# Moving the FFN's DMA transposes to ScalarE's queue, two more tiles by DMA, and split scores for dilation one

## The chip, the cores and the metric

The kernel runs on one core of a Trainium2 chip. The metric is the time of one launch on the device in microseconds, taken as the median of several runs. One more run was profiled; all rows below come from it.

## What is computed

A trunk of two layers over 256 tokens of width 1024: a sparse attention mixer (NSA) and an FFN, then a dilated attention mixer and an FFN, each with a norm ahead, a norm behind and a residual sum. The parts that matter here, from the reference:

```python
def swiglu(h, w_gu, w_down):
    gu = h @ w_gu
    g, u = gu[..., :D_FF], gu[..., D_FF:]
    return (jax.nn.silu(g) * u) @ w_down

# dilated_mixer: for each (window, dil) of ((128, 1), (512, 4), (2048, 16))
    q = partial_rope(proj[:, :, gi, 0], cos, sin)
    k = partial_rope(proj[:, :, gi, 1], cos, sin)
    v = proj[:, :, gi, 2]
    o, lse = banded_attention(to_residue(q, dil)[:, :, :, None], to_residue(k, dil),
                              to_residue(v, dil), window // dil)
...
    s = jnp.einsum('nqhgd,nkhd->nhgqk', qc, kc).astype(jnp.float32) * scale
```

## The kernel before

Everything is written out by hand: five engine programs (SyncE, GpSimd, ScalarE, VectorE, TensorE), each in a fixed order, tied by semaphores. Tokens come in two tiles of 128, m = 0 and 1. A weight piece (128 x 2048 floats) is loaded by SyncE into a ring of seven slots; ScalarE copies it to a rounded high part `w_hi` (line 719, two halves), VectorE subtracts to get `w_lo` (line 1231), and each product is three single-pass matmuls, hi·hi, hi·lo and lo·hi (`three`, all matmuls at line 1785). Small matmuls of plain float operands (scores, values) are left in full float and are issued by the same helper `mm`.

**FFN.** The hidden width 2816 is cut into FJ = 11 tiles j = 0 to 10. For each (j, m) TensorE makes gate and up (`gu`), ScalarE the silu (986), VectorE the product `hs` (1569). `hs` must be transposed before the down projection can use it. For j = 2 to 9 (`XBAR`) that goes by DMA: GpSimd splits the floats into two 16-bit planes (679), SyncE's queue issues a DMA transpose (474, in `turn_planes`, placed among the weight loads by `turns_before`), GpSimd merges the planes into `ht` (684). For j = 0, 1 and 10 TensorE transposes instead (`ht_turn`, line 1794). ScalarE then copies the high part to `st_hi` (998, `ht_out`; `end_hi` for j = 10), VectorE makes `st_lo` (1575), and TensorE runs `down`. TensorE's order of a step is gu(j, 0), down(j-1, 0), gu(j, 1), down(j-1, 1). The last step is gu(10, 0), down(9, 0) with the transposes of hs(10, 0) in its middle, down(10, 0), gu(10, 1), down(9, 1), down(10, 1).

**Dilated attention.** The heads are taken in four groups g of four. The tiles of a group (projections of q and k for each of the three dilations, `pat` 0 to 2, and of the values) follow each other; in between stand the attention steps of the group before, two heads (a pair) at a time, 16 pairs in all. A q/k tile is evacuated by ScalarE (1079), rotated by VectorE (`dil_rope`, 1663 to 1670), transposed by TensorE (`dil_turn`) into bank 2 or 3, and copied by ScalarE to `qk_t` (1102 to 1111). `dil_scores` makes the scores of a pair: for dilation one a 64x128 by 64x256 product per head in full float, and eight 64x64 products for the other two. VectorE masks (1426), ScalarE takes the exponential (901), VectorE normalises (`norm_unit`, 1459), TensorE transposes the probabilities (`dil_turn_probs`).

Of the kernel before, what the change touches and what calls it, by code (L numbers as in the profile page):

```python
# [39 lines left out]
P = 128  # L40
# [83 lines left out]
N_TURNS = sum(x.kind == QK for x in TILES)  # L124

# [68 lines left out]
def build(nc, x, positions, norm_mix_pre, norm_mix_post, norm_ffn_pre, norm_ffn_post, ffn_w_gu,  # L194
# [3 lines left out]
    with ctx:  # L198
# [25 lines left out]
        probs = sb("probs", [P, 4, 512], at=at_tmp)  # L224
        pair = sb("pair", [P, 2, HK, S], at=at_tmp)
# [211 lines left out]
        rope_parts = sem("rope_parts")  # L437
# [32 lines left out]
        def _(sp):  # L470
            def turn_planes(layer, j, m):

                sp.wait_ge(planes_ready, xbar_no(layer, j, m) + 1)
                sp.dma_start_transpose(planes_t[:, j % 2, m, :, :], planes[:, j % 2, m, :])\
                  .then_inc(planes_turned[m], 16)

            def turns_before(n):

                for layer, first in enumerate((N_FFN0, N_FFN1)):
                    for j in XBAR:  # L480
                        if n == first + 3 * j + 6:
# [2063 lines left out]
```

## Time and profile before

| | us |
|---|---|
| median of 3 runs | 815.26 (815.19 to 816.67) |
| the profiled execution, its own time | 814.93 |
| its span, first to last instruction | 812.9 |
| TensorE matmul busy | 801.4 (99%), 4377 instructions |
| VectorE busy | 511.5 (63%) |
| ScalarE busy | 455.5 (56%) |
| GpSimd busy | 96.7 (12%) |

2.03 us of the profiled execution lie outside its span. TensorE's granted clock was 0.998 of full speed over the span. Matmuls are pipelined, so two of them overlap in the records: a 512-column matmul is recorded with 0.39 us, but the next one starts some 0.23 us after it. What a matmul costs is therefore read from start to start, and idle time from the starts as well.

### The profile page before, as it was taken

How to read it: one execution, taken by the hardware profiler on the slowest of the kernel's cores; microseconds unless marked ns; L12 is line 12 of the kernel's file. 1: busy time of each engine (PE TensorE's matmuls, PEld its weight loads, DVE VectorE, ACT ScalarE, POOL GpSimd, SP SyncE). 2: the span in 40 equal slices, each digit the busy share in tenths (PEclk: the TensorE clock that was granted, in tenths of full speed). 3: DMA queues.
4: the chain of work that ended last, by engine and by line, in shares of the span. 5: the costliest groups of instructions: out<-in, count | busy, mean ns of one | idle time of the engine just before them, and what ended most of it. 6: DMA issues, size and time to landing. Idle time of an engine off the chain costs nothing.

```text
span 812.9 us, 11748 instructions
## 1 busy us (share of the span) xinstructions
PE 801.4 (99%) x4377; PEld 643.5 (79%) x4377; DVE 511.5 (63%) x1073; ACT 455.5 (56%) x879; POOL 96.7 (12%) x159
## 2 busy tenths in 40 slices
PE   9999999999999999999999999999999999999996
PEld 7877675788888888788877878878877888888885
DVE  5966979786646464686565665666568765555444
ACT  7836878764535353575555666555558553535331
POOL 1000005700222222000000000000000012222210
PEclk9999999999999999999999999999999999999999
DMA  9955211166986687558444535363434667767711
GB/s 318 346 186 197 88 54 53 63 223 195 234 216 191 191 244 216 170 194 273 153 160 145 167 115 197 104 206 105 156 110 142 196 226 203 207 184 238 224 32 52
DMA packets 126312, 141.69 MB, mean 174 GB/s; under 512 B 23680, under 2 KB 109744, under 8 KB 126128
## 3 DMA queue, kind: packets, MB, share of 16 engines
q1 hardware_dynamic: 125168, 136.73, 54.6%
q0 software_dynamic: 992, 4.19, 1.3%
q8 instruction: 35, 0.57, 0.3%
q14 instruction: 21, 0.17, 0.1%
q10 hardware_dynamic: 96, 0.02, 0.0%
HBM read 134.64 MB, written 2.10 MB: 168 GB/s over the span
## 4 chain that ended last, share of the span: by engine, by line
PE 83%; DMA 6%; issue 4%; POOL 3%; DVE 2%; ACT 1%; POOLq 0%; ACTq 0%; DVEq 0%
PE ps L1785 73%; PE ps L1794 6%; DMA planes_t<-planes 6%; POOL ht L684 2%; PE ps L2062 2%; PE ps L2035 2%; POOL planes L679 1%; PE ps L1847 1%; PE ps L2073 1%; ACT junk L740 0%; ACT xd_hi L728 0%; DVE w_lo L1231 0%; DVE h L1555 0%; DVE h L1561 0%; DVE tmp L1559 0%
## 5 line engine op out<-in xcount | busy, mean ns | idle before, releaser
L1231 DVE TENSOR_TENSOR w_lo<-w_raw,w_hi 128x1024 fp32r<-128x1024 f32 x240 | 288.5, 1229 | 73.3 <-ACT w_hi L719 71.0
L719 ACT ACTIVATE w_hi<-w_raw 128x1024 fp32r<-128x1024 f32 x240 | 246.1, 1061 | 2.9 <-DMA w_raw<-in_ffn_w_gu 2.7
L1785 PE MATMUL ps<-w_hi,xt_hi 128*128 128x512 f32 x472 | 188.8, 401 | 0.0
L1785 PE MATMUL ps<-w_hi,xt_lo 128*128 128x512 f32 x472 | 183.6, 390 | 0.0
L1785 PE MATMUL ps<-w_lo,xt_hi 128*128 128x512 f32 x472 | 183.0, 390 | 0.0
L1785 PE MATMUL ps<-w_hi,xd_hi 128*128 128x512 f32 x288 | 117.4, 408 | 0.2 <-DVE w_lo L1231 0.2
L1785 PE MATMUL ps<-w_hi,xd_lo 128*128 128x512 f32 x288 | 113.2, 393 | 0.0
L1785 PE MATMUL ps<-w_lo,xd_hi 128*128 128x512 f32 x288 | 112.8, 392 | 0.0
L1785 PEld LDWEIGHTS ps<-w_hi,xt_hi 128*128 128x128 f32 x472 | 88.5, 188 | 24.5 <-issue 8.2
L986 ACT ACTIVATE silu<-ps,rs 128x256 f32<-128x256 f32 x44 | 20.9, 474 | 151.2 <-PE ps L1785 151.1
L1785 PEld LDWEIGHTS ps<-w_hi,xt_lo 128*128 128x128 f32 x472 | 88.6, 188 | 18.8
L1785 PEld LDWEIGHTS ps<-w_lo,xt_hi 128*128 128x128 f32 x472 | 88.7, 188 | 16.6 <-DVE w_lo L1231 0.3
L1569 DVE SCALAR_TENSOR_TENSOR hs<-ps,rs,silu 128x256 f32<-128x256 f32 x44 | 21.2, 483 | 107.3 <-ACT silu L986 107.3
L1785 PEld LDWEIGHTS ps<-w_hi,xd_lo 128*128 128x128 f32 x288 | 54.7, 190 | 11.8
L1785 PEld LDWEIGHTS ps<-w_hi,xd_hi 128*128 128x128 f32 x288 | 54.8, 190 | 10.9 <-DVE w_lo L1231 0.4
L1785 PEld LDWEIGHTS ps<-w_lo,xd_hi 128*128 128x128 f32 x288 | 54.9, 191 | 9.8
L1785 PE MATMUL ps<-w_hi,st_hi 128*128 128x512 f32 x160 | 62.6, 391 | 0.0
L1785 PE MATMUL ps<-w_hi,st_lo 128*128 128x512 f32 x160 | 62.3, 389 | 0.0
L1785 PE MATMUL ps<-w_lo,st_hi 128*128 128x512 f32 x160 | 62.3, 389 | 0.0
L684 POOL COPY ht<-planes_t 128x512 uint16<-128x512 uint16 x32 | 37.3, 1167 | 121.1 <-DMA planes_t<-planes 121.1
L679 POOL COPY planes<-hs 128x512 uint16<-128x512 uint16 x32 | 22.8, 713 | 129.5 <-DVE hs L1569 129.5
L1785 PEld LDWEIGHTS ps<-w_hi,st_lo 128*128 128x128 f32 x160 | 30.0, 188 | 6.3
(259 smaller groups left out, 936.0 us busy)
## 6 DMA issues: line engine op xcount, KB each, us to landing
w_raw<-in_ffn_w_gu SPq DMA_DIRECT2D x88, 512.0 KB, 5.1
w_raw<-in_dil_w_in SPq DMA_DIRECT2D x72, 512.0 KB, 4.6
w_raw<-in_ffn_w_down SPq DMA_DIRECT2D x44, 512.0 KB, 4.9
w_raw<-in_nsa_w_in SPq DMA_DIRECT2D x20, 512.0 KB, 7.3
w_raw<-in_nsa_w_o SPq DMA_DIRECT2D x8, 512.0 KB, 4.7
w_raw<-in_dil_w_o SPq DMA_DIRECT2D x8, 512.0 KB, 4.4
w_k<-in_nsa_cmp_wk SPq DMA_DIRECT2D x2, 1024.0 KB, 9.1
w_raw<-in_nsa_cmp_wv SPq DMA_DIRECT2D x2, 1024.0 KB, 11.6
```

Of the source, the lines that this page charges most:

```text
L679: pool.tensor_copy(view(planes, at, [[256, 2], [1, 256]]), halves_of(hs[:, m, :]))\
L684: pool.tensor_copy(halves_of(ht[:, j % 2, m, :]), view(planes_t, at, [[256, 2], [1, 256]]))\
L719: act.activation(w_hi[:, n.slot, c:c + 1024], w_raw[:, n.slot, c:c + 1024], ACT.Copy)\
L986: act.activation(silu[:, m, :], bank(gu_bank(j, m), 0, 256), ACT.Silu, scale=rs[:, m:m + 1])\
L1231: dve.tensor_tensor(w_lo[:, n.slot, c:c + 1024], w_raw[:, n.slot, c:c + 1024], w_hi[:, n.slot, c:c + 1024].bitcast(F32), ALU.subtract)\
L1569: dve.scalar_tensor_tensor(hs[:, m, :], bank(gu_bank(j, m), 256, 256), rs[:, m:m + 1], silu[:, m, :], ALU.mult, ALU.mult).then_inc(hs_read ...
L1785: ins = pe.matmul(o, s, m, start=start, stop=stop, **kw)
L1794: ins = pe.transpose(ps[0:n, b, P * k:P * k + P], src, ident[:, 0:P])
L1847: pe.transpose(bank(3, 0, P), ident[:, 0:P], ident[:, 0:P])
L2035: pe.matmul(bank(score_bank(odd), 0, 2 * n), q_t[rows, hd // 2, m * P:(m + 1) * P], k_both[rows, :, hd // G, 0:n], start=True, stop=True). ...
L2062: pe.matmul(view(ps, OT_BANK * 512 + P * j, [[1, P]], p0=DH * odd, n=DH), v_nsa[:, i // (m + 1), i % (m + 1), hk * DH:(hk + 1) * DH], p_t2 ...
L2073: ins = pe.matmul(bank(OT_BANK, P * j, P), vc_bd[:, r, P * j:P * j + P], pc_t[:, 2 * r + m, :], start=False, stop=True, skip_group_check=True)
```

## The change

Four things.

1. **Issuer.** The DMA transposes leave SyncE's program. ScalarE issues them, each after a wait for its planes: that of (j-1, 1) after the first weight piece of step j, that of (j, 0) after the first half of its third piece. GpSimd's code is the same work cut into `split_hidden` and `merge_hidden`.
2. **Two more tiles.** `XBAR` becomes a list that also holds (1, 0) and (1, 1), so TensorE's `ht_turn` is left only for j = 0 and 10. `ht_out(1, 0)` moves behind `silu_step(1, 1)` on ScalarE and behind `hs_step(1, 1)` on VectorE.
3. **The last step.** `ht_out(9, 1)` moves behind `ht_out(10, 0)` on both engines.
4. **Scores.** For dilation one ScalarE writes the transposed q and k rounded (`qk_hi`), VectorE writes the rest from PSUM (`dil_turn_lo`, six instructions for each of eight tiles) and TensorE makes three rounded products per head. The 64x64 products come first. The order of the dilations becomes 1, 2, 0 in the first group and 1, 0, 2 in the others. `dil_turn` waits for `qk_lo_ready` before it writes a bank over. Since `qk_lo` lies partly in `g_post`, GpSimd loads `g_post` for the dilated layer's norm only when all scores are done.

```diff
-XBAR = range(2, FJ - 1)
+XBAR = [(1, 0), (1, 1)] + [(j, m) for j in range(2, FJ - 1) for m in range(MT)]
...
@@ def _(sp):
-            def turn_planes(layer, j, m):
-
-                sp.wait_ge(planes_ready, xbar_no(layer, j, m) + 1)
-                sp.dma_start_transpose(planes_t[:, j % 2, m, :, :], planes[:, j % 2, m, :])\
-                  .then_inc(planes_turned[m], 16)
...
@@ def _(pool):
-                    pool.wait_ge(proj_done[1], LAST_E)
+                    pool.wait_ge(scores[1], 8 * DIL_G)
                     post_gain(b + 1, *nexts[b])
...
@@ def _(act):
+                def turn_planes(j, m):
+
+                    act.wait_ge(planes_ready, xbar_no(layer, j, m) + 1)
+                    act.dma_start_transpose(planes_t[:, j % 2, m, :, :], planes[:, j % 2, m, :])\
+                      .then_inc(planes_turned[m], 16)
...
                 def step(j, nx):
 
                     split(nx)
+                    turn_planes(j - 1, 1)
                     split(nx + 1, (0,))
                     silu_step(j, 0)
                     split(nx + 1, (1,))
                     split(nx + 2, (0,))
+                    turn_planes(j, 0)
                     ht_out(j - 1, 1)
...
                 j, nx = FJ - 1, Piece(n0 + 3 * FJ - 1)
                 split(nx)
-                ht_out(j - 1, 1)
+                turn_planes(j - 1, 1)
                 split(nx + 1, (0,))
                 silu_step(j, 0)
                 split(nx + 1, (1,))
                 ht_out(j, 0)
                 split(nx + 2, (0,))
+                ht_out(j - 1, 1)
                 post_squares(b + 1, 0)
...
@@ def _(dve):
+            def dil_turn_lo(x):
+
+                if x.kind != QK or x.pat:
+                    return
+                dve.wait_ge(turn_out[1], x.qk_no + 1)
...
+                for hp in range(2):
+                    for par in range(2):
+                        to, dims = 32 * x.m + P * par, [[64, 2], [1, 32]]
+                        dve.scalar_tensor_tensor(view(qk_lo[hp], to, dims), view(ps, src + P * hp + par, [[2, 2], [4, 32]]),
+                                                 -SCALE, view(qk_hi, at + hp * S + to, dims).bitcast(F32),
+                                                 ALU.mult, ALU.subtract)
+                for hp in range(2):
+                    to, dims = x.m * 64, [[P, 2], [1, 64]]
+                    ins = dve.tensor_tensor(view(qk_lo[2 + hp], to, dims), view(ps, src + (2 + hp) * P, [[1, 2], [2, 64]]),
+                                            view(qk_hi, at + (2 + hp) * S + to, dims).bitcast(F32), ALU.subtract)
+                ins.then_inc(qk_lo_ready, 1)
...
                 dil_attend(2 * e, True)
                 dil_attend(2 * e + 1, False)
+                dil_turn_lo(TILES[e - 1])
...
@@ def _(pe):
-                    gu(j, 1, pc, mid=(lambda: ht_turn(1, 1)) if j == 2 else None)
+                    gu(j, 1, pc)
...
-                ht_turn(1, 0)
+                pe.wait_ge(hs_ready, ffn_order(layer, 1, 0) + 1)
...
-                for odd, w in enumerate(ws):
-                    j = 2 * hp + odd
-                    mm(bank(score_bank(w), 0, S), head(g, 0, 0, j, m * P, P), head(g, 0, 1, j, 0, S), True, True)
...
+                for j, w in zip(js, ws):
+                    mm(bank(score_bank(w), 0, S), first_hi(g, 0, j, m * P, P), first_hi(g, 1, j, 0, S), True, False)
+                for j, w in zip(js, ws):
+                    mm(bank(score_bank(w), 0, S), first_hi(g, 0, j, m * P, P), first_lo(1, j, 0, S), False, False)
+                for j, w in zip(js, ws):
+                    mm(bank(score_bank(w), 0, S), first_lo(0, j, m * P, P), first_hi(g, 1, j, 0, S), False, True)\
+                        .then_inc(scores[1], 1)
```

ScalarE at the end of the first FFN, before: `st_hi<-ht` right after the two `w_hi` is `ht_out(9, 1)`, the silu after it that of (10, 0).

```order
L986 ACTIVATE silu<-ps,rs 128x256
L998 ACTIVATE st_hi<-ht 128x2x128
L719 ACTIVATE w_hi<-w_raw 128x1024 x2
L998 ACTIVATE st_hi<-ht 128x2x128
L719 ACTIVATE w_hi<-w_raw 128x1024
L986 ACTIVATE silu<-ps,rs 128x256
L719 ACTIVATE w_hi<-w_raw 128x1024
L998 ACTIVATE end_hi<-ps 128x2x128
L719 ACTIVATE w_hi<-w_raw 128x1024
```

The same engine and place now:

```order
L1002 ACTIVATE silu<-ps,rs 128x256
L1012 ACTIVATE st_hi<-ht 128x2x128
L735 ACTIVATE w_hi<-w_raw 128x1024 x2
L1018 DMA_TRANSPOSE planes_t<-planes 128x4x128
L735 ACTIVATE w_hi<-w_raw 128x1024
L1002 ACTIVATE silu<-ps,rs 128x256
L735 ACTIVATE w_hi<-w_raw 128x1024
L1012 ACTIVATE end_hi<-ps 128x2x128
L735 ACTIVATE w_hi<-w_raw 128x1024
L1012 ACTIVATE st_hi<-ht 128x2x128
```

The `st_hi` that stood ahead of the silu of (10, 0) stands behind `end_hi`; in its old place ScalarE issues the DMA transpose of (9, 1).

TensorE at the first pair of scores, in the middle of a projection (`w_` and `xd_` are its operands), before:

```order
L1785 MATMUL ps<-w_lo,xd_hi 128x512
L1785 MATMUL ps<-w_hi,xd_lo 128x512
L1785 MATMUL ps<-qk_t 128x256 x2
L1785 MATMUL ps<-qk_t 64x64 x8
L1785 MATMUL ps<-w_hi,xd_hi 128x512
```

and now:

```order
L1830 MATMUL ps<-w_hi,xd_lo 128x512
L1830 MATMUL ps<-qk_t 64x64 x8
L1830 MATMUL ps<-qk_hi 128x256 x2
L1830 MATMUL ps<-qk_lo_110,qk_hi 128x256 x2
L1830 MATMUL ps<-qk_hi,qk_lo_108 128x256 x2
L1830 MATMUL ps<-w_hi,xd_hi 128x512
```

Two products of 128x256 became six, and the eight small ones stand ahead of them.

VectorE in the same stage, where a tile of dilation one has just been transposed and a pair has just been scored (`mn` belongs to the mask), before:

```order
L1426 ISA probs,mn<-ps,mask_dil 128x384
L1426 ISA mn 128x1
L1231 TENSOR_TENSOR w_lo<-w_raw,w_hi 128x1024
L1663 TENSOR_TENSOR rope_a<-stage_dil,cos_106 128x128
L1664 TENSOR_TENSOR rope_b<-stage_dil,sin_107 128x8x8
L1666 TENSOR_TENSOR rope_b<-stage_dil,sin_107 128x8x8
L1670 TENSOR_TENSOR stage_dil<-rope_a,rope_b 128x8x16
L1457 RECIPROCAL rl<-l_u 128x1
L1459 TENSOR_SCALAR probs<-probs,rl 128x384
```

and now:

```order
L1451 ISA probs_dil_59,mn<-ps,mask_dil 128x384
L1451 ISA mn 128x1
L1708 SCALAR_TENSOR_TENSOR qk_lo_108<-ps,qk_hi 128x2x32 x2
L1708 SCALAR_TENSOR_TENSOR qk_lo_109<-ps,qk_hi 128x2x32 x2
L1713 TENSOR_TENSOR qk_lo_110<-ps,qk_hi 128x2x64
L1713 TENSOR_TENSOR qk_lo_111<-ps,qk_hi 128x2x64
L1256 TENSOR_TENSOR w_lo<-w_raw,w_hi 128x1024
L1688 TENSOR_TENSOR rope_a<-stage_dil,cos_115 128x128
```

Six instructions came in between the masks and the next `w_lo`; the rotation and the normalisation behind them keep their order.

## Rows read from the trace of the kernel before

**Rows 1.** Busy time by stage; columns: stretch, length, PE, PEld, DVE, ACT, POOL, clock.

```profile
220.00:328.00 108.00, 106.54 (x472) 87.99 (x471) 57.62 (x67) 48.11 (x66) 24.48 (x26) 1.00 0.77 213
390.00:580.00 190.00, 190.00 (x1207) 153.15 (x1206) 111.72 (x233) 109.83 (x215) 0.00 (x0) 1.00 0.48 155
```

**Rows 2.** Two PE transposes of hs(1, 1), order of time; columns: start, length.

```profile
199.33 0.38 PE L1794 MATMUL ps<-ident,hs 128*128 128x128 f32 x2
199.46 0.48 PE L1785 MATMUL ps<-w_hi,xt_hi 128*128 128x512 f32 x1
```

**Rows 3.** One FFN step, ACT and POOL, in order of time.

```profile
219.50 3.17 ACT L719 ACTIVATE w_hi<-w_raw 128x1024 fp32r<-128x1024 f32 x3
219.94 0.74 POOL L679 COPY planes<-hs 128x512 uint16<-128x512 uint16 x1 [3.23 <-DVE hs L1569]
```

**Rows 4.** The tile planes_t: issue in ns (min/median/max), then microseconds to landing.

```profile
L474 SPq DMA_TRANSPOSE planes_t<-planes x32: 1190/1197/1826, 195.8 to 782.6; - x32
...
DMA to landing us min/median/max: 2.4/2.7/6.3
```

**Rows 5.** End of the first FFN, in order of time; brackets: idle before, releaser.

```profile
324.47 0.39 PE L1785 MATMUL ps<-w_hi,xt_lo 128*128 128x512 f32 x1
324.60 0.42 ACT L998 ACTIVATE st_hi<-ht 128x256 fp32r<-128x256 f32 x1 [5.18 <-POOL ht L684]
...
325.87 0.45 ACT L986 ACTIVATE silu<-ps,rs 128x256 f32<-128x256 f32 x1
...
327.53 1.21 DVE L1231 TENSOR_TENSOR w_lo<-w_raw,w_hi 128x1024 fp32r<-128x1024 f32 x1
327.67 0.44 PE L1794 MATMUL ps<-ident,hs 128*128 128x128 f32 x2 [1.46 <-DVE hs L1569]
...
329.34 0.40 PE L1785 MATMUL ps<-w_hi,end_hi 128*128 128x512 f32 x1
```

**Rows 6.** End of the second FFN, the same place.

```profile
788.42 0.39 PE L1785 MATMUL ps<-w_hi,xt_lo 128*128 128x512 f32 x1
...
788.85 0.47 ACT L986 ACTIVATE silu<-ps,rs 128x256 f32<-128x256 f32 x1 [2.57 <-PE ps L1785]
789.42 0.48 DVE L1569 SCALAR_TENSOR_TENSOR hs<-ps,rs,silu 128x256 f32<-128x256 f32 x1 [2.69 <-ACT silu L986]
```

**Rows 7.** A pair's scores on PE and PEld, read in short windows.

```profile
409.78 0.19 PEld L1785 LDWEIGHTS ps<-qk_t 64*128 64x128 f32 x2 [0.36 <-issue]
409.89 0.19 PEld L1785 LDWEIGHTS ps<-qk_t 64*128 64x128 f32 x2
410.11 0.38 PE L1785 MATMUL ps<-qk_t 64*128 64x256 f32 x2
410.42 0.15 PEld L1785 LDWEIGHTS ps<-qk_t 64*64 64x64 f32 x4 [0.33 <-issue]
```

**Rows 8.** Rounded matmuls of 256 columns, two neighbours among 24 of the gates.

```profile
29.17 0.28 PE L1785 MATMUL ps<-xt_hi,gw_lo 128*128 128x256 f32 x1
29.29 0.28 PE L1785 MATMUL ps<-xt_hi,gw_hi 128*128 128x256 f32 x1
```

**Rows 9.** DVE: durations from PSUM (ns min/median/max), then a wait (us in total, times, longest).

```profile
L1279 DVE SCALAR_TENSOR_TENSOR xt_lo<-ps,g_t,xt_hi x48: 336/341/352, 8.2 to 635.3; 128x128 fp32r<-128x128 f32 x48
...
DVE rope_a L1663 <- ACT stage_dil L1079: 17.4, 16, 2.3
```

**Rows 10.** A normalisation and the transposes that wait for it, in order of time.

```profile
576.87 0.42 DVE L1459 TENSOR_SCALAR probs<-probs,rl 128x384 f32<-128x384 f32 x1
577.55 0.49 PE L1794 MATMUL ps<-ident,probs 128*128 128x128 f32 x3
```

**Rows 11.** Last scores, first use of g_post; then the page's row of that load.

```profile
606.75 1.09 PE L1785 MATMUL ps<-qk_t 64*128 64x256 f32 x20
...
613.72 0.68 DVE L1540 TENSOR_TENSOR tmp<-ps,g_post 128x512 f32<-128x512 f32 x1
...
g_post<-in_norm_mix_post POOLq DMA_DIRECT2D x2, 512.0 KB, 4.8
```

More of the change, by code:

```diff
@@ L80, with qk_order @@
 QK, V01, V2 = "qk", "v01", "v2"
+def qk_order(g):
+    return (1, 2, 0) if g == 0 else (1, 0, 2)
 def dil_chunks(g):
-    qk = [(QK, p) for p in range(3)]
+    qk = [(QK, p) for p in qk_order(g)]
     if g == 0:
@@ L111, in dil_tiles, with xbar_of @@
     return tiles
-XBAR = range(2, FJ - 1)
+XBAR = [(1, 0), (1, 1)] + [(j, m) for j in range(2, FJ - 1) for m in range(MT)]
 def xbar_no(layer, j, m):
-    return MT * (len(XBAR) * layer + j - XBAR[0]) + m
+    return len(XBAR) * layer + XBAR.index((j, m))
+def xbar_of(layer, j, m):
+    tiles = [x for x in XBAR if x[1] == m]
+    return len(tiles) * layer + tiles.index((j, m)) + 1
 TILES = dil_tiles()
@@ L124, with firsts_until @@
 N_TURNS = sum(x.kind == QK for x in TILES)
+def firsts_until(qk_no):
+    return sum(x.kind == QK and x.pat == 0 and x.qk_no <= qk_no for x in TILES)
 def pair_start(g, t):
@@ L224, in build @@
         probs = sb("probs", [P, 4, 512], at=at_tmp)
+        probs_dil = [sb(f"probs_dil{i}", [P, DIL_N], at=at_tmp + i // 2 * 4096 + i % 2 * 4 * DIL_N) for i in range(4)]
         pair = sb("pair", [P, 2, HK, S], at=at_tmp)
@@ L281, in build @@
         p_t2 = sb("p_t2", [P, 2, 512], at=at_s + 4096)
+        qk_lo = [sb(f"qk_lo{i}", [P, S], F32R, at=at) for i, at in
+                 enumerate((at_gp + 3072, at_s + 9216, at_tmp + 3072, at_tmp + 7168))]
         mask_nsa = sb("mask_nsa", [P, 2 * P], BF16, at=at_s + 9216)
@@ L899, in exp_unit @@
                     act.wait_ge(normed[1], w - 3)
-                p = probs[:, w % 4, 0:DIL_N]
+                p = probs_dil[w % 4][:, :]
                 act.activation(p, p, ACT.Exp, bias=mn[:, w % 4, 0:1], scale=-1.0,
@@ L1022, in ffn @@
                 split(Piece(n0 + 5))
+                turn_planes(1, 0)
                 act.wait_ge(rs_ready[b], 2)
                 silu_step(0, 1)
-                ht_out(1, 0)
                 split(Piece(n0 + 6))
@@ L1028, in ffn @@
                 silu_step(1, 1)
+                ht_out(1, 0)
                 split(Piece(n0 + 7))
@@ L1457, in norm_unit @@
                 link(dve.reciprocal(rl[:, w % 4, 0:1], l_u[:, w % 4, 0:1]))
-                p = probs[:, w % 4, 0:DIL_N]
+                p = probs_dil[w % 4][:, :]
                 dve.tensor_scalar(p, p, rl[:, w % 4, 0:1], None, ALU.mult).then_inc(normed[1], 1)
@@ L1598, in ffn @@
                 hs_step(0, 1)
-                ht_out(1, 0)
                 split(Piece(n0 + 6))
@@ L1602, in ffn @@
                 hs_step(1, 1)
+                ht_out(1, 0)
                 split(Piece(n0 + 7))
@@ L1608, in ffn @@
                 split(nx)
-                ht_out(j - 1, 1)
                 split(nx + 1, (0,))
@@ L1614, in ffn @@
                 split(nx + 2, (0,))
+                ht_out(j - 1, 1)
                 gain_post(2 + 2 * layer, 0)
@@ L1677, in dil_mask @@
                         dve.wait_ge(pt_psum[1], w - 3)
[L1678 removed]
+                    mask_part(probs_dil[w % 4][:, :], w, 0, DIL_N, mask_dil[:, dil_unit(t)[0], :],
                               mn[:, w % 4, 0:1])\
@@ L2401, in dil_turn_probs @@
                 for k in range(3):
-                    ins = turn(PT_BANK, k, probs[:, w % 4, P * k:P * k + P])
+                    ins = turn(PT_BANK, k, probs_dil[w % 4][:, P * k:P * k + P])
                 ins.then_inc(pt_psum[1], 1)
```

92 lines of the change are left out of this document (49 added, 43 removed).

## The prediction

> **What bounds the kernel now.** I read the busy time by stage first. TensorE is busy for 190.00 of 190 us in the dilated stage and for 106.54 of 108 us in the first FFN, at a clock of 1.00, while ScalarE is busy for 48.11 and VectorE for 57.62 of the 108 [rows 1]. So the time is TensorE's instruction stream plus the few places where that stream waits, and a change counts only where it shortens the one or fills the other. The chain of waits names DMA transposes all through the FFN, but TensorE has no gap there: 472 matmuls in 106.54 us are 0.226 us each [rows 1], and neighbours start that far apart all along, so that part of the chain is not a bound. In order of time I then looked for gaps between the starts of TensorE's matmuls. Outside the launch and the tail there is one over half a microsecond, at the end of the first FFN, where the transposes of hs(10, 0) start late, with 1.46 us of idle time ahead of them [rows 5]. The second FFN has the same code there and no gap: its silu starts 0.43 us after the start of the last gate matmul and its hs 0.57 us behind that [rows 6].
>
> **The change part by part.** Changes are set against the profiled execution, 814.93 us, of which the span is 812.9; the median of the three runs, 815.26, is 0.33 above it.
>
> *Transposes that TensorE no longer makes.* hs(1, 0) and hs(1, 1) in two layers are four pairs of transposes. After the start of a pair the next matmul starts 0.13 us later [rows 2], so a pair costs 0.13 and the four 0.52 us, all on the path. TensorE keeps its wait for hs(1, 0), which it also had before, since the bank is written over. In place of the pair stand GpSimd's two copies, a DMA and ScalarE's issue. The result is wanted by down(1, 0) and down(1, 1) only after a further 60 matmuls or more, 13.6 us at 0.226; planes 0.74 [rows 3], issue to landing at most 6.3 [rows 4] and two short copies fit in that. **-0.5 us.**
>
> *The issue on ScalarE.* An issue occupied SyncE for 1.2 us, 1.83 at the longest [rows 4]; ScalarE has no row of a transpose, and I take 1.2. In an FFN step there are two, 2.4 us (at most 3.7). A step is 72 matmuls of 0.226, 16.3 us, in which ScalarE is busy for 48.11/108, 7.3 us, so 9.0 are idle [rows 1]. The new wait stands ahead of `w_hi` copies and of `ht_out`, so these are queued behind it, and through them VectorE's `w_lo` and TensorE. Does it wait? The planes of (j, 1) are ready at 219.94 + 0.74 = 220.68, and ScalarE comes to the issue after two of three `w_hi` that began at 219.50 and take 3.17 together, at 221.6 [rows 3]. It does not. What is late next is `ht_out` by some 1.2 us; TensorE wants (j, 1) only 72 matmuls after its gate, 16.3 us, against 1.7 + 6.3 + copies. The weights are split a whole step ahead. SyncE's loads lose a wait, which nobody on the path feels. **0**; the bounds are a small gain from earlier loads, under 0.2, and the third rival.
>
> *The end of the first FFN.* ScalarE waited 5.18 us for ht(9, 1), then copied it at 324.60, then one `w_hi`, and only then made the silu of (10, 0) at 325.87 [rows 5]. With `ht_out(9, 1)` moved behind, the silu starts as in the second FFN, at 324.47 + 0.43 = 324.90, hs 0.57 later at 325.47, and it ends by 325.95 [rows 5, 6]. TensorE is at that point at 324.47 + 7 x 0.226 = 326.05 (one gate matmul and six of down), so hs is in time and the gap of 327.67 - 326.05 = 1.6 us closes. What is late next is `end_lo`: VectorE makes a `w_lo` of 1.21 us ahead of it, which started 1.66 us after the silu [rows 5]. 324.90 + 1.66 + 1.21 + 0.4 for `end_lo` itself is 328.2. TensorE wants it 1.67 us (329.34 - 327.67) after the transposes [rows 5], at 327.7. So 0.4 to 0.5 comes back; I take 0.4. **-1.2 us** (-1.6 if nothing comes back, -0.3 if another 0.9 does). The second FFN has no gap there to give.
>
> *Scores.* A pair's two heads run side by side on the two halves of the array. In full float a pair loads weights at 409.78, loads again at 409.89, starts its second pair of matmuls at 410.11 and hands over at 410.42 [rows 7]. That is 0.11 for the first load, two streams of 0.213 (256 columns, twice each, at 2.4 GHz) and 0.10 to drain: 0.64. The second load ran beside the first stream and cost nothing. Now there are three streams of a single pass. Rounded matmuls of 256 columns with a new weight each start 0.12 us apart [rows 8], though on the whole array. So 0.11 + 3 x 0.12 + 0.10 = 0.57, 0.07 less, in 16 pairs: **-1.1 us.** The number of switches of tile shape stays. Bounds: the loads of each stream stay visible, 0.11 + 0.12 per stream, which makes 3 x 0.23 - 0.43 = +0.26 per pair, +4.2 us; or the two heads don't overlap, 6 x 0.12 - 0.43 = +0.29, +4.6 us. I take the first value, since rows 7 show the hidden load in this very shape.
>
> The page "TensorE: Matmul & The Clock Gate" of the Trainium skill, section "Part 3: Packing small matmuls — row/col tiling", says that a weight load overlaps a running matmul only where the two use other row groups. Here both loads go to the same two halves and the trace shows the overlap, so it disagrees; by that sentence the scores would cost +4.2 us and not -1.1.
>
> *VectorE's new work.* A batch is four instructions of 64 columns and two of 128. From PSUM, 128 columns took 0.341 us [rows 9]; six of them are 2.0 us, the upper bound of a batch, and eight batches 16 us. In the 190 us of the dilated stage VectorE has 78 idle [rows 1]. A batch delays the next `w_lo`, which is made pieces ahead, and the next rotation, ahead of which VectorE idled 17.4/16 = 1.1 us on average [rows 9]. The tightest reader is TensorE's transpose of probabilities: a normalisation at 576.87 of 0.42 us ends 0.26 before the transposes at 577.55 [rows 10]. The batch can start only when ScalarE has copied the tile, and the old program waited in the same place for ScalarE's next `w_hi`, so about half of it fills idle time. **0**, at most +3.8 (second rival).
>
> *`g_post`* is asked for after the last scores, 606.75 + 1.09 = 607.84, lands 4.8 later at 612.6 and is used at 613.72 [rows 11]. **0**, with 1.1 to spare.
>
> Sum: -0.5 - 1.2 - 1.1 = -2.8. 814.93 - 2.8 = 812.1 for a profiled execution; with the 0.33, **812.4** as a median.
>
> **The rivals.**
> 1. *The loads of the rounded scores stay visible* (slower). For it: no row shows rounded products on half the array, and a load of 128 columns is as long as a stream of 256 in one pass, so there is no margin. Against: rows 7 and 8. It decides as soon as a stream costs over 0.18 us: 0.43/3 = 0.143 is break-even for the scores alone, and 1.7/48 = 0.035 on each of the 48 streams eats the gains of the other parts. At 0.23 it is -1.7 + 4.2 = +2.5: 817.7.
> 2. *VectorE becomes late in the dilated stage.* Six batches have pairs in flight. Each can be late by 2.0 less the 1.1 of idle time less the slack of 0.26, 0.64 us: 6 x 0.64 = +3.8, net +1.0: 816.3. For it: the slack of 0.26. Against: the batch overlaps a wait that VectorE had.
> 3. *ScalarE's queue is held by the transposes* (slower). It decides when issues and waits exceed the 9.0 us that are idle in a step; every microsecond beyond is paid in some 18 steps, so 10 us a step is 815 + 18 = 833. Against: the sums above.
> 4. *The change does less than it says at the end of the FFN*: the gap moves to `end_lo` or the following steps, and the scores break even. -0.5 - 0.3 = -0.8: 814.5.
>
> **How the numbers follow.** About 0.2% (1.63 us) is what a measurement of this kernel can tell from no change, so faster means below 813.6 and slower above 816.9. Forecast 0.58 (812.4, own range 811.2 to 813.6), rival 1 0.11, rival 2 0.15, rival 3 0.05, rival 4 0.11. Faster 0.58; same, rivals 2 and 4, 0.26; slower, rivals 1 and 3, 0.16. The range takes the forecast down to 811.0 (the whole 1.6 at the FFN's end and some gain from the loads) and up over rivals 4 and 2 to 816.6, which leaves out rivals 1 and 3.
>
> **What would show it.** In the trace after: TensorE's idle time before the transposes of hs(10, 0) in the first FFN gone or under 0.5 us; a pair's scores from the first load to the next projection 0.07 shorter, with weight loads that start beside running matmuls; no idle time of TensorE before transposes of probabilities; DMA_TRANSPOSE rows on ScalarE's queue of about 1.2 us, and FFN matmuls still 0.226 apart. It is wrong if rounded streams on half the array start over 0.14 us apart, if TensorE waits for `probs` or `stage_dil`, or if 0.226 grows.

## The result and the profile after

| us | before | changed | difference |
|---|---|---|---|
| median, 6 runs each, side by side | 815.23 | 810.86 | ratio 0.9944, 95% interval 0.9931 to 0.9957: -5.6 to -3.5 |
| the profiled execution | 814.93 | 810.76 | -4.17 |
| its span | 812.9 | 809.0 | -3.9 |
| the same comparison on another chip (16 and 5 runs) | 814.9 | 811.05 | ratio 0.9949, 0.9937 to 0.9962 |

The kernel became faster by 4.4 us where 2.8 had been forecast; 810.86 lies 0.14 below the range's low end. Every part went in the direction forecast, and the forecast was too small. The parts inside the span come to 3.5 us; where the rest of the 4.4 lies is told under "What is left".

The windows of the changed kernel over the stretches of [rows 1] (columns: stretch, length, PE, PEld, DVE, ACT, POOL, clock, share of DMA, GB/s):

```profile
220.00:328.00 108.00, 107.88 (x477) 88.90 (x477) 62.03 (x68) 51.12 (x69) 23.58 (x27) 1.00 0.76 210
390.00:580.00 190.00, 190.00 (x1237) 155.31 (x1236) 117.00 (x271) 111.16 (x218) 0.00 (x0) 1.00 0.48 155
```

TensorE is now busy for 107.88 of the 108 us of the FFN, against 106.54, with 477 instructions in place of 472: the hole at the end is nearly gone. In the dilated stage it stays full, with 1237 recorded instructions for 1207: each of the 12 pairs in the stretch has 22 instead of 20 (a full-float product is recorded as two, so four became six), and as the pairs take less time, a few more fit in.

The FFN matmuls around 199 us, where [rows 2] had the transposes of hs(1, 1), order of time:

```profile
199.21 0.39 PE L1830 MATMUL ps<-w_hi,xt_lo 128*128 128x512 f32 x1
199.43 0.39 PE L1830 MATMUL ps<-w_hi,xt_hi 128*128 128x512 f32 x1
199.66 0.39 PE L1830 MATMUL ps<-w_lo,xt_hi 128*128 128x512 f32 x1
```

They are 0.227 apart without a break. The end of the first FFN, answering [rows 5], on ScalarE, VectorE and TensorE:

```profile
324.07 0.47 ACT L1002 ACTIVATE silu<-ps,rs 128x256 f32<-128x256 f32 x1 [2.77 <-PE ps L1830]
...
325.53 1.23 DVE L1256 TENSOR_TENSOR w_lo<-w_raw,w_hi 128x1024 fp32r<-128x1024 f32 x1 [0.39 <-ACT w_hi L735]
326.67 0.42 DVE L1600 TENSOR_TENSOR end_lo<-ps,end_hi 128x256 fp32r<-128x256 f32 x1
...
325.00 0.39 PE L1830 MATMUL ps<-w_hi,st_lo 128*128 128x512 f32 x1
325.23 0.39 PE L1839 MATMUL ps<-ident,hs 128*128 128x128 f32 x2
...
326.63 0.40 PE L1830 MATMUL ps<-w_hi,st_lo 128*128 128x512 f32 x1
327.14 0.51 PE L1830 MATMUL ps<-w_hi,end_hi 128*128 128x512 f32 x1
```

The silu waits for TensorE alone, the transposes start 0.23 after the matmul ahead of them, and 0.28 us come back (326.63 to 327.14, less 0.227): VectorE's `w_lo` ends late and `end_lo` with it, as forecast. The matmul behind, at 327.48 in the trace, adds 0.11 (0.34 after 327.14 instead of 0.227), so that 0.39 come back where 0.4 was taken.

A pair of scores, answering [rows 7], on TensorE and its weight loads:

```profile
407.70 0.46 PE L1830 MATMUL ps<-qk_t 64*64 64x64 f32 x16
408.10 0.39 PE L1830 MATMUL ps<-qk_hi 64*128 64x256 f32 x2
408.32 0.28 PE L1830 MATMUL ps<-qk_lo,qk_hi 64*128 64x256 f32 x2
408.44 0.28 PE L1830 MATMUL ps<-qk_hi,qk_lo 64*128 64x256 f32 x2
408.64 0.51 PE L1830 MATMUL ps<-w_hi,xd_hi 128*128 128x512 f32 x1
...
408.09 0.18 PEld L1830 LDWEIGHTS ps<-qk_hi 64*128 64x128 f32 x2
408.20 0.19 PEld L1830 LDWEIGHTS ps<-qk_lo,qk_hi 64*128 64x128 f32 x2
408.32 0.19 PEld L1830 LDWEIGHTS ps<-qk_hi,qk_lo 64*128 64x128 f32 x2
```

The second and third loads start 0.11 and 0.12 apart, beside the running products, and the rounded part takes 0.55 from its first load to the next projection. A sentence of the Trainium skill ("TensorE: Matmul & The Clock Gate", section "Part 3: Packing small matmuls — row/col tiling") lets a load overlap only with a matmul on other row groups; by it each stream would show its load. These rows disagree with it, as [rows 7] did.

One row moved that the prediction had not looked for. The tile of the DMA transposes, with the landing in its last line (issue to landing), answering [rows 4]:

```profile
L1018 ACTq DMA_TRANSPOSE planes_t<-planes x36: 1205/1207/1293, 174.3 to 779.1; - x36
...
DMA to landing us min/median/max: 2.4/6.1/9.1
```

An issue on ScalarE takes 1.21 us, as taken. But the median landing went from 2.7 to 6.1 us. A median hides two groups here. Before, from step 2 on, the tiles with m = 0 landed in 2.4 to 2.8 us and those with m = 1 in 4.6 to 6.3; now they take 2.4 to 5.3 and 6.0 to 8.6, and the four tiles of step 1 take 6.3 to 9.1. (In every trace the last tile of the program, with no load beside it, lands in 2.4; it is left out of these ranges.)

**Where the time went.** The start of the same instruction in each trace, in us after its start in the changed kernel (e1 to e13 are the experiments below; silu(j, m) is the silu of hidden tile j and token tile m). The first row is ahead of everything that was changed, so it is only where that execution stood when it began; what counts is how a column moves from one row to the next.

| | before | e1 | e2 | e3 | e4 | e13 |
|---|---|---|---|---|---|---|
| first silu, first FFN | 0.36 | -0.48 | -0.17 | 0.10 | 0.11 | 0.30 |
| silu(3, 0), both pairs of step 1 past | 0.83 | -0.52 | 0.30 | 0.06 | 0.07 | 0.26 |
| silu(10, 0) | 1.80 | 4.82 | 0.73 | 0.37 | 0.07 | 0.44 |
| silu(10, 1) | 2.08 | 7.37 | 0.73 | 0.36 | 0.06 | 0.89 |
| first pair of scores | 2.09 | 7.29 | 0.69 | 0.33 | -0.06 | 0.87 |
| last pair of scores | 3.29 | 7.26 | 0.67 | 1.55 | -0.07 | 0.82 |
| first silu, second FFN | 3.42 | 7.32 | 0.72 | 1.70 | -0.06 | 0.88 |
| last silu | 3.90 | 7.24 | 1.18 | 2.15 | -0.09 | 0.84 |

Column "before" splits the 3.9 us of the span: 0.36 at the launch, which no edit touches; 0.47 and 0.48 for the transposes of step 1 in the two FFNs; 0.97 and 0.28 at the end of the first; 1.34 in the dilated stage. The change itself is 3.5. The 0.97 and 0.28 belong together, as both come from the waits around the last step.

### The profile page after: what moved, and what is told of

It reads as the page before. It is cut to its first block, busy times and chain, and to the rows that moved or that the text cites. A ratio compares the mean times of both kernels' runs of the same rounds, so it can differ in the third digit from the quotient of the medians.

```text
span 809.0 us, 11869 instructions
## 1 busy us (share of the span) xinstructions
PE 798.6 (99%) x4401; PEld 643.8 (80%) x4401; DVE 528.5 (65%) x1121; ACT 457.5 (57%) x879; POOL 102.2 (13%) x167
## 4 chain that ended last, share of the span: by engine, by line
PE 96%; DVE 2%; ACT 1%; issue 0%; POOL 0%; ACTq 0%; POOLq 0%
PE ps L1830 86%; PE ps L1839 6%; PE ps L2107 2%; PE ps L2080 2%; PE ps L2118 1%; PE ps L1892 1%; ACT junk L756 0%; DVE w_lo L1256 0%; ACT xd_hi L744 0%; ACT w_hi L735 0%; ACT probs_b L907 0%; DVE h L1580 0%; DVE h L1586 0%; DVE tmp L1584 0%; ACT p_t L922 0%
## 5 line engine op out<-in xcount | busy, mean ns | idle before, releaser
L1256 DVE TENSOR_TENSOR w_lo<-w_raw,w_hi 128x1024 fp32r<-128x1024 f32 x240 | 295.5, 1259 | 64.8 <-ACT w_hi L735 62.5
L691 POOL COPY ht<-planes_t 128x512 uint16<-128x512 uint16 x36 | 33.4, 928 | 212.1 <-DMA planes_t<-planes 212.1
L1012 ACT ACTIVATE st_hi<-ht 128x256 fp32r<-128x256 f32 x36 | 15.0, 416 | 70.8 <-PE ps L1830 42.1
L1600 DVE TENSOR_TENSOR st_lo<-ht,st_hi 128x256 fp32r<-128x256 f32 x36 | 15.2, 422 | 48.2 <-ACT st_hi L1012 48.2
```

Of the source, the lines that this page charges most:

```text
L691: pool.tensor_copy(halves_of(ht[:, j % 2, m, :]), view(planes_t, (j % 2 * MT + m) * 512, [[256, 2], [1, 256]])).then_inc(ht_merged, 1)
L1012: act.activation(view(st_of(j)[0], m * P, [[S, 2], [1, P]]), ht_from(j, m), ACT.Copy)\
L1256: dve.tensor_tensor(w_lo[:, n.slot, c:c + 1024], w_raw[:, n.slot, c:c + 1024], w_hi[:, n.slot, c:c + 1024].bitcast(F32), ALU.subtract)\
L1600: dve.tensor_tensor(view(st_of(j)[1], m * P, [[S, 2], [1, P]]), ht_from(j, m), hi.bitcast(F32), ALU.subtract).then_inc(ht_ready, 1)
```

## The experiments

Each edit is made in the changed kernel. The expectations compare with its 810.9; the kernel before, beside them, had medians of 814.7 to 814.9.

**e1: the end of the FFN in its old order.**

```diff
 # last step, ScalarE (VectorE likewise)
+ht_out(j - 1, 1)
 split(nx + 1, (0,))
 silu_step(j, 0)
 ...
 split(nx + 2, (0,))
-ht_out(j - 1, 1)
```

The table of this order that the waits use (`ht_order`) is put back with it.

> The changed kernel with one thing undone: in the last step of an FFN the copy of ht(9, 1), on ScalarE and VectorE, stands again ahead of the silu of (10, 0). Theory A, that this order is worth 1.25 us: TensorE idles about 1.5 us ahead of the transposes of hs(10, 0) in the first FFN again, and the kernel takes 1.2 to 1.3 us more than the changed one, some 812.1 us. Theory B, that the gap closed because the transposes were issued and landed at other times and not through the order: silu(10, 0) still comes 0.4 us after the last gate matmul, the gap stays under 0.4 us, and the time stays at 810.9. The second FFN shows no change under either.

Measured: 817.41 us, ratio to before 1.0029 (1.0018 to 1.0041): slower than the kernel before. Neither theory had that size. ScalarE and TensorE at the place:

```profile
318.20 1.21 ACTq L1018 DMA_TRANSPOSE planes_t<-planes  x1
...
327.62 0.42 ACT L1012 ACTIVATE st_hi<-ht 128x256 fp32r<-128x256 f32 x1 [7.62 <-POOL ht L691]
327.94 1.04 ACT L735 ACTIVATE w_hi<-w_raw 128x1024 fp32r<-128x1024 f32 x1
328.89 0.46 ACT L1002 ACTIVATE silu<-ps,rs 128x256 f32<-128x256 f32 x1
...
330.69 0.69 PE L1839 MATMUL ps<-ident,hs 128*128 128x128 f32 x2 [5.81 <-DVE hs L1594]
331.03 0.78 PE L1830 MATMUL ps<-w_hi,st_hi 128*128 128x512 f32 x1
331.60 0.63 PE L1830 MATMUL ps<-w_lo,st_hi 128*128 128x512 f32 x1
```

ScalarE stands 7.62 us before ht(9, 1), whose transpose was issued at 318.20, and the silu of (10, 0) behind it waits too. TensorE then idles for 5.81 us, and its matmuls start 0.43 apart instead of 0.23. The windows of this kernel (columns as above) say why:

```profile
300.00:324.00 24.00, 24.00 (x107) 19.90 (x106) 11.83 (x14) 9.80 (x13) 4.94 (x6) 1.00 0.83 232
324.00:331.00 7.00, 1.19 (x6) 0.69 (x5) 2.41 (x4) 2.67 (x4) 0.75 (x1) 0.84 0.33 69
331.00:336.00 5.00, 5.00 (x15) 3.95 (x14) 2.41 (x3) 1.33 (x2) 0.00 (x0) 0.54 0.00 0
336.00:345.00 9.00, 9.00 (x42) 7.36 (x41) 5.83 (x16) 3.19 (x7) 0.00 (x0) 1.00 0.41 127
```

The granted clock is 1.00 ahead of the idle time and 0.54 behind it, close to the lower of its two levels (1.2 of 2.4 GHz), though TensorE is busy throughout; from 336 on it is 1.00 again. From its transposes at 330.69 to the matmul that starts at 335.77 TensorE takes 5.08 us, and the same instructions at the fast spacing (0.15, 0.32, then ten of 0.23) would take 2.8. These 2.3 us are most of the 2.55 by which e1's column grows from silu(10, 0) to silu(10, 1). So theory A names the place, and the size depends on when the transpose lands.

**e11: the old order, with SyncE issuing.** The edit is that of e1 made in e4 (below).

> Transposes issued by SyncE as in e4, and ht(9, 1) copied ahead of the silu of (10, 0) as in e1: the two undone together. In e1 the old order cost 6.5 us and not 1.25, with the transpose of (9, 1) landing 8.6 us after its issue on ScalarE. Theory A, that the order alone is worth 1.2 to 1.3 us and that the rest of e1 is the late landing on ScalarE's queue: 812.0 us, a gap of about 1.5 us ahead of the transposes of hs(10, 0), matmuls after it 0.23 us apart. Theory B, that the old order costs some 6 us in the changed program whoever issues: 817 us.

Measured: 812.66 us, ratio 0.9974 (0.9966 to 0.9983), 1.9 above e4; the trace shows it too:

```profile
324.33 0.42 ACT L1028 ACTIVATE st_hi<-ht 128x256 fp32r<-128x256 f32 x1 [5.84 <-POOL ht L707]
...
327.41 0.44 PE L1845 MATMUL ps<-ident,hs 128*128 128x128 f32 x2 [2.11 <-DVE hs L1600]
```

Theory A: a gap of 2.11 us, and no slow matmuls behind it (starts at 327.92, 328.15 and 328.38). The same order costs 1.25 us in the profiled execution of before, 1.9 here and 7.8 in that of e1 (6.6 by e1's median). It is one mechanism whose price is how late ht(9, 1) is; with the issue on ScalarE the new order is needed, not just useful.

**e4: SyncE issues again.**

```diff
 # SyncE, at the old places among the loads
+sp.wait_ge(planes_ready, xbar_no(layer, j, m) + 1)
+sp.dma_start_transpose(planes_t[:, j % 2, m, :, :], planes[:, j % 2, m, :])
 # ScalarE
-turn_planes(j - 1, 1)
-turn_planes(j, 0)
```

> The changed kernel with all DMA transposes issued by SyncE's queue again, at the places among the loads where the kernel before had them; the rest is as in the changed kernel. Theory A, that the issuer is worth nothing to the time: 810.9 us within 0.3, FFN matmuls 0.2266 us apart in both. Theory B, that part of the result beyond the three other edits comes from SyncE's freed queue (earlier loads): up to 0.8 us slower than the changed kernel, 811.7 us, with waits of ScalarE or TensorE for w_raw or w_lo. On the landing (median 2.7 us from issue before, 6.1 after): if it is the queue, or loads that run while SyncE is not held, it goes back to about 2.7 us here; if it is what ScalarE does, it stays near 6.

Measured: 810.73 us, ratio 0.9948 (0.9935 to 0.9962); in the table its column never leaves the changed kernel's by over 0.11. Theory A: in this execution the issuer alone moves nothing. The landing of the tile:

```profile
DMA to landing us min/median/max: 2.4/4.5/7.5
```

The median didn't go back to 2.7, but the landings did: from step 2 on the tiles with m = 0 land in 2.4 us (two in 3.8 and 4.4) and those with m = 1 in 4.5 to 5.7, as before. The four tiles of step 1, which the kernel before didn't send by DMA, land in 5.0 to 7.5 and move the median from one group to the other.

**e10: ScalarE issues, and SyncE holds its loads until the transpose has landed.**

```diff
 # SyncE, ahead of the load at the old place of each transpose
+sp.wait_ge(planes_turned[m], 16 * xbar_of(layer, j, m))
```

> The changed kernel (transposes on ScalarE's queue), but SyncE holds its next weight loads until each transpose has landed, at the places where the kernel before issued them. Theory A, that the landing of 6 to 9 us comes from weight loads that are in flight beside the transpose: the median landing falls to about 2.5 us. Theory B, that it is ScalarE's queue itself: it stays near 6 us. The loads come up to 4 us later; as weights are split a step (16.3 us) ahead, the time stays at 810.5 to 811; if that slack is used up, FFN steps grow and the time goes over 813.

Measured: 810.51 us, ratio 0.995 (0.9935 to 0.9965). The landing:

```profile
DMA to landing us min/median/max: 2.4/4.6/10.6
```

The queue is still ScalarE's, and from step 2 on the tiles with m = 0 land in 2.4 to 4.9 us and those with m = 1 in 4.5 to 6.6, where the changed kernel has 6.0 to 8.6. So the late landing is made mainly by weight loads in flight and not by the queue itself. Theory A's 2.5 is not reached, because the loads ahead of the held one are still moving: one issued at 218.53 lands at 224.60, and the transpose issued at 219.50 lands at 225.15, 5.7 us after its issue. The first tile of step 1 still takes 10.6. Holding the loads cost nothing.

**e2: step 1 on TensorE again.**

```diff
-XBAR = [(1, 0), (1, 1)] + [(j, m) for j in range(2, FJ - 1) for m in range(MT)]
+XBAR = [(j, m) for j in range(2, FJ - 1) for m in range(MT)]
```

with the two pairs of transposes put back into TensorE's program, and the first split of GpSimd back to its old place.

> The changed kernel with hs(1, 0) and hs(1, 1) transposed by TensorE again, two pairs in each FFN. Theory A, that a pair costs what it delays the matmul after the next one, 0.25 us: the rows of each FFN come 0.5 us later, 1.0 us in all, 811.9 us. Theory B, that a pair costs the 0.13 us from its start to the next matmul's, as the prediction had it: 0.26 us per FFN, 0.52 in all, 811.4 us, and then half a microsecond of the result has another source.

Measured: 811.79 us, ratio 0.9961 (0.9948 to 0.9973). In the table the pairs add 0.47 by silu(3, 0) and 0.46 between the first and last silu of the second FFN, 0.93 to 1.0 in all: theory A. Another 0.43 comes at the end of the first FFN, where nothing was edited. There, on GpSimd, ScalarE and TensorE:

```profile
312.73 0.76 POOL L691 COPY ht<-planes_t 128x512 uint16<-128x512 uint16 x1 [10.05 <-DMA planes_t<-planes]
313.41 0.61 POOL L683 COPY planes<-hs 128x512 uint16<-128x512 uint16 x1
...
314.05 1.21 ACTq L1015 DMA_TRANSPOSE planes_t<-planes  x1
315.36 0.42 ACT L1009 ACTIVATE st_hi<-ht 128x256 fp32r<-128x256 f32 x1 [4.94 <-issue]
...
315.78 0.39 PE L1827 MATMUL ps<-w_hi,xt_lo 128*128 128x512 f32 x1
316.29 0.50 PE L1827 MATMUL ps<-w_hi,st_hi 128*128 128x512 f32 x1
```

TensorE waits 0.28 us for the copy of ht(8, 1), whose merge on GpSimd began 10.0 us after the transpose's issue at 302.72; in the changed kernel's own profile the same one took 7.8. The late landing is only a part of it. The merge is done at 313.49, but the copy starts only at 315.36: GpSimd splits (9, 0) only after that merge, and ScalarE issues the transpose of (9, 0) ahead of the copy, so 0.6 us of split and 1.2 of issue come in between. With SyncE issuing, nothing of this stands ahead of the copy.

**e5: 32 spare pairs of transposes.**

```diff
 # TensorE, FFN steps 2 to 9, between the halves of each gate product
+turn(6 + m, 0, ident[:, 0:P])
+turn(6 + m, 1, ident[:, 0:P])
```

> The changed kernel with 32 pairs of transposes of the identity added, two in each of the eight middle steps of both FFNs, between the two halves of the gate matmuls; nothing waits for them. Theory A, that a pair costs 0.25 us: +8.0 us, 818.6. Theory B, that it costs the 0.13 us up to the next matmul's start: +4.2 us, 814.8.

Measured: 818.93 us, ratio 1.0051 (1.0037 to 1.0065): 8.1 us more for 32 pairs, 0.25 each; theory A. In the trace the 16 pairs of the first FFN shift its silus by 4.05, 0.253 each. One of them:

```profile
190.52 0.39 PE L1830 MATMUL ps<-w_hi,xt_lo 128*128 128x512 f32 x1
190.75 0.38 PE L1839 MATMUL ps<-ident 128*128 128x128 f32 x2
190.89 0.48 PE L1830 MATMUL ps<-w_hi,xt_hi 128*128 128x512 f32 x1
191.20 0.39 PE L1830 MATMUL ps<-w_lo,xt_hi 128*128 128x512 f32 x1
191.43 0.40 PE L1830 MATMUL ps<-w_hi,xt_lo 128*128 128x512 f32 x1
```

The next matmul starts 0.14 after the pair, but the one behind it follows 0.31 later instead of 0.227. At the last matmul shown the shift is 0.23; the other 0.02 of the 0.253 come behind it.

**e3: full-float scores again, without VectorE's batches.**

```diff
-mm(..., first_hi(g, 0, ...), first_hi(g, 1, ...), True, False)
-mm(..., first_hi(g, 0, ...), first_lo(1, ...), False, False)
-mm(..., first_lo(0, ...), first_hi(g, 1, ...), False, True)
+mm(..., head(g, 0, 0, ...), head(g, 0, 1, ...), True, True)
 # VectorE
-dil_turn_lo(TILES[e - 1])
```

> The changed kernel with the scores of dilation one in full float again, one product per head after the eight small ones, and without VectorE's eight batches of low parts. Theory A, that a pair of scores is 0.083 us shorter in three rounded streams and that the batches cost nothing: the dilated stage is 1.3 us longer than in the changed kernel, 812.2 us. Theory B, that the streams gain more and that the batches take some of it back: less than 1.3 us longer, 811.5 us or less. Theory C, that the gain comes from the new order (small products first) and not from the streams: the stage is as long as in the changed kernel, 810.9 us.

Measured: 812.53 us, ratio 0.9972 (0.9961 to 0.9984). The dilated stage is 1.34 us longer (0.36 to 1.70 in the table), evenly over the pairs: theory A, 0.08 a pair, with nothing given back by the batches. Theory C falls: the new order is kept here, and the stage is as long as in the kernel before (its column grows by the same 1.34). The remaining 0.8 of this profile are two waits for late transposes as in e2 (0.29 and 0.47, one in each FFN, both for ht(8, 1), landing after 9.8 and 9.9 us).

**e6: one product per head in place of three** (leaves out the two products with low parts).

```diff
-mm(..., first_hi(g, 0, ...), first_lo(1, ...), False, False)
-mm(..., first_lo(0, ...), first_hi(g, 1, ...), False, True)
```

> The changed kernel with one rounded product per head in the scores of dilation one in place of three (leaves out the two products with the low parts, so the scores are coarser; VectorE's batches stay). Theory A, that a stream of a head pair costs 0.12 us: 32 streams fewer, -3.8 us, 806.8. Theory B, that each stream keeps its weight load in sight, 0.23 us: -7.4 us, 803.2. Theory C, that the streams hide behind a wait of the pair (masks, probabilities): under -1.5 us.

Measured: 806.64 us, ratio 0.99 (0.9887 to 0.9914), -4.2 us. From the first to the last pair, 15 of them, its trace gains 3.45 us, 0.115 per stream: theory A. All 32 streams make 3.7 of the 4.2; in the trace, its first silu also came 0.51 before the changed kernel's, which no edit explains.

**e7: more work on ScalarE.**

```diff
 # ScalarE, FFN steps 2 to 9: three of the six w_hi copies made twice
-split(nx)
+split(nx, twice=True)
-split(nx + 1, (1,))
+split(nx + 1, (1,), twice=True)
```

> The changed kernel with three more w_hi copies (1.05 us each, made twice) on ScalarE in each of the 16 middle FFN steps, two of them ahead of the issue of the transpose of (j - 1, 1). Theory A, that only ScalarE's idle time in a step counts (16.3 us less 7.3 less 2.4 leaves 6.6 for 3.2 more): 810.9 us. Theory B, that what counts is the time from planes to TensorE's use, of which a landing of 7.8 us leaves some 2.5: issues 2.1 us later use it up, TensorE waits ahead of down(j - 1, 1) in many steps, 0.3 to 1 us each, 815 to 827 us.

Measured: 811.69 us, ratio 0.9962 (0.9949 to 0.9975), 0.6 to 0.8 above the changed kernel. ScalarE works 51 us more (508.6 against 457.5) and the FFN steps don't move; the trace loses half a microsecond at one place, the end of the first FFN, where a `w_lo` of 1.72 us (1.23 in the changed kernel) ends at 327.56 and `end_lo` starts behind it, 0.82 later than there (0.32 of this is the launch). Theory A for the steps, then. Theory B failed because issues that come later land sooner; for most tiles with m = 1 the trace has three loads in flight just behind the issue, where the changed kernel has four:

```profile
DMA to landing us min/median/max: 2.4/4.5/9.1
```

**e8: VectorE's batches three times over.**

```diff
-for hp in range(2): ...   # six instructions
+for again in range(3): for hp in range(2): ...
```

> The changed kernel with each of VectorE's eight batches of low parts in the dilated stage made three times over instead of once. Theory A, that VectorE has room: a batch (six instructions, under 2.0 us) delays the next w_lo and the next rotation by 4 us more, and as w_lo is pieces ahead, TensorE doesn't feel it: 810.9 us. Theory B, that the slack of 0.26 us ahead of the transposes of probabilities decides, as the second rival had it: each of six batches with pairs in flight makes TensorE wait 2 to 4 us, 823 to 835 us.

Measured: 814.22 us, ratio 0.9992 (0.9983 to 1.0001): 3.2 to 3.4 us above the changed kernel, most of the gain. VectorE, then TensorE:

```profile
447.53 1.21 DVE L1256 TENSOR_TENSOR w_lo<-w_raw,w_hi 128x1024 fp32r<-128x1024 f32 x1
...
449.77 0.42 DVE L1484 TENSOR_SCALAR probs_dil<-probs_dil,rl 128x384 f32<-128x384 f32 x1
...
450.25 0.44 PE L1842 MATMUL ps<-ident,probs_dil 128*128 128x128 f32 x2 [1.05 <-DVE probs_dil L1484]
```

Theory B has the mechanism, TensorE waiting for probabilities, and theory A is wrong that VectorE has room without end. B's size is too large: two such waits of over 1 us, which shift the pairs behind them by 1.26 and 1.28, and two shifts of some 0.4, not six of 2 to 4.

**e13: the changed kernel once more**, unedited, on another chip.

> The changed kernel itself, unedited, on the same chip and beside the same runs of the kernel before as e12. Theory A, that ScalarE's queue costs some tenths in some executions through landings of up to 10 us: 0.1 to 0.5 us slower than the same program with SyncE's queue, and a first FFN whose (9, 1) or (8, 1) copy comes late in this profile or not. Theory B, that the issuer is worth nothing: 810.7 us, as e4.

Measured: 811.05 us, and a profiled span of 809.8 against 809.0. The table shows where: 0.18 and 0.45 at the end of the first FFN. VectorE and TensorE there:

```profile
321.59 0.43 DVE L1600 TENSOR_TENSOR st_lo<-ht,st_hi 128x256 fp32r<-128x256 f32 x1 [3.48 <-ACT st_hi L1012]
322.54 3.50 DVE L1256 TENSOR_TENSOR w_lo<-w_raw,w_hi 128x1024 fp32r<-128x1024 f32 x3 [0.53 <-ACT w_hi L735]
325.96 0.48 DVE L1594 SCALAR_TENSOR_TENSOR hs<-ps,rs,silu 128x256 f32<-128x256 f32 x1
...
326.49 0.44 PE L1839 MATMUL ps<-ident,hs 128*128 128x128 f32 x2 [0.66 <-DVE hs L1594]
```

A copy of a late transpose holds VectorE, three `w_lo` pile up behind it, and hs(10, 0) is late. So late landings cost 0.6 us in this execution and nothing in the first. The profiles of e2, e3 and e6, which issue on ScalarE too, lose 0.3 to 0.8 each to such waits for ht(8, 1); those with SyncE issuing and the new order (e4, e12) lose nothing in their steps. Theory A in the traces; as medians, 811.05 and e4's 810.73 were not taken beside each other and are too close to part.

**e12: a version meant to beat both**: e4, and VectorE makes `end_lo` first.

```diff
 hs_step(j, 0)
+ht_out(j, 0)
 split(nx + 1, (1,))
-ht_out(j, 0)
 split(nx + 2, (0,))
```

> A version meant to beat both: transposes issued by SyncE as in e4, and in the last step of an FFN VectorE makes end_lo ahead of the w_lo half that stood before it. Theory A: the 0.28 us for which TensorE waits ahead of its first matmul with end_hi, in the first FFN, go away, and the 0.11 of the slower matmul behind it with them: -0.3 to -0.4 us against e4 in the trace, 810.4 us. Theory B: the next wait (the w_lo half, or the copies behind) takes their place: 810.7 us, no change in the trace.

Measured: 810.63 us (809.95 to 810.71), ratio 0.9942 (0.9929 to 0.9954), beside e13's 811.05 (810.62 to 811.6). TensorE at the place:

```profile
326.92 0.40 PE L1836 MATMUL ps<-w_hi,st_lo 128*128 128x512 f32 x1
327.15 0.39 PE L1836 MATMUL ps<-w_hi,end_hi 128*128 128x512 f32 x1
```

0.23 apart: the 0.28 is gone, theory A. Counted from the first silu, silu(10, 1) comes 0.43 earlier than in e4, of which 0.27 is left at the last silu. It beats the kernel before by 0.58%; against the changed kernel the gain is shown by the trace, and the intervals of the ratios overlap.

## Why the prediction was too small

*The transposes of step 1: -0.5 forecast, -0.95 to -1.0 measured.* This is the step that failed. It read the price of a pair from its start to the next matmul's (0.13) and stopped too early. In [rows 2] that next matmul, at 199.46, has 0.48 us where its neighbours have 0.39, and the trace of before goes on with a start 0.32 later and not 0.227:

```profile
199.78 0.39 PE L1785 MATMUL ps<-w_lo,xt_hi 128*128 128x512 f32 x1
```

The 0.13 and this 0.09 make 0.22, and the last 0.03 is spread over the transposes' own start and the matmuls further on. e5 gives 0.253 a pair, e2 confirms it in place. The price of such a pair is the shift of the steady rhythm some instructions on, not the distance to the next start.

*The scores: -1.1 forecast, -1.3 measured.* The mechanism was right to the loads that hide; 0.07 a pair was 0.083. A stream is 0.115 (e6), 0.12 was taken. The first rival, visible loads, is refuted by e6 (its 0.23 per stream would have given 7.4 us there).

*The end of the first FFN: -1.2 forecast, -1.25 measured* in the profiled executions, with 0.39 of the 0.4 coming back at `end_lo`. The order was the cause, as forecast (e1). The size was in part luck: it hangs on one landing of the profiled execution of before, and the same order cost 1.9 and 7.8 elsewhere (e11, e1).

*The issue on ScalarE: 0 forecast; 0 in one trace, 0.6 lost in another (e13).* A second step that failed, though it is not what made the forecast too small. The sums of idle time stand (e7), and the third rival, 10 us a step, is far off. But the step took SyncE's landing of at most 6.3 us over to another queue. SyncE had held its own loads while it waited for `planes`, and every second of its transposes landed in 2.5 us; ScalarE's go out beside the loads (e10) and land after up to 10 us, which uses up the slack at the end of the FFN. It also looked at the issue of (j, 1) alone for a wait: that of (j, 0) does wait, for a split that GpSimd makes only after merging (j - 1, 1), and stands ahead of the copy of (j - 1, 1) (e2). In small, that is the third rival's mechanism: 0.3 to 0.8 us in the traces that show it (e2, e3, e6, e13).

*VectorE's batches: 0 forecast, 0 measured* (e3: an even 0.08 a pair). A batch is 1.4 us by its rows (four of 0.215, two of 0.281), not the bound of 2.0. The second rival's mechanism is real, and thrice the work brings it out (e8). *`g_post`*: nothing lost, the first silu of the second FFN keeps the gain.

*The fourth rival* fell: the gap at the end closed.

*What is left.* The parts measured make 3.5 us, and the spans agree: 812.7 in the median of 42 runs of before, 809.2 in 11 of the changed kernel. Set against the 2.8, step 1 gave 0.4 to 0.5 more, the scores 0.2 and the end of the FFN nothing much. The other 0.9 of the 4.4 lies outside these parts. About 0.3 is time outside the span, which the prediction took as unchanged: 2.01 to 2.12 us in all 42 runs of before, 1.69 to 1.80 in the 11 of the changed kernel. It goes with the program and not with chance: e3, which undoes the scores, has 1.91 to 2.01, e11, which undoes the issuer and the order at the end, 1.79 to 2.28, and the other edits have 1.69 to 1.85. Its cause stays open. The rest, 0.5 to 0.6, is scatter between series of runs: the median of 815.23 comes from six runs, and the 42 have 814.73, against which the changed kernel's 11, at 810.95, are 3.8 faster. In the profiled pair the launch alone makes 0.36, and the first silus of all the kernels lie between 165.70 and 166.62. The range's low end left room for a mis-sized part but none for this, though three runs of before, from 815.19 to 816.67, showed the scatter.

## What to carry to other kernels

Price a small instruction between large matmuls by how far the steady rhythm some instructions later is shifted, not by the next start. When a DMA moves to another queue, ask which transfers the old queue held back while it waited: its landing time belonged to that order, not to the transfer. Ask as well what stands behind the issue in the new engine's program: here it was the copy that TensorE wanted next. Ahead of a copy that waits for a DMA put nothing that TensorE needs sooner: the same old order cost 1.25, 1.9 and 7.8 us, depending on one landing. And where half a microsecond matters, take more than three runs of the kernel before: their median was 0.5 above that of 42.

## What the runs showed of the hardware

- A DMA transpose of 128x512 landed in 2.4 to 2.5 us after its issue in nearly every case where no weight load was in flight beside it, and in 4.3 to 10.6 with four or more in flight between issue and landing (to 7.8 at most on SyncE's queue).
- After a pair of 128x128 transposes the second matmul starts 0.31 to 0.32 after the first, not 0.227; the first matmul after half-array scores is 0.51 long and its successor 0.34 to 0.35 behind it.
- After 5.81 us of idle time TensorE's granted clock was 0.54 over 331 to 336 (matmuls 0.43 apart, though it was busy all the while) and 1.00 again from 336 on; after 2.11 us of idle time (e11) the matmuls stayed 0.23 apart.
- Rounded 64x256 products with a new weight each start 0.115 apart on half the array, as close as the full array's in [rows 8].
- The time outside the span was 2.05 us in the median for the kernel before and 1.75 for the changed one, run after run.
